# TensorE's program for 32 expert blocks written out without its loop

## The reference

```
p_g, g_idx = top_k(softmax(x @ w_group + b_group), 1)            # 1 of 4 groups
top_vals, top_idx = top_k(logits of the 8 experts of that group, 2)
weights = p_g * softmax(top_vals)
for each expert e of 32:  a, b = split(x @ w_gate_up[e], 2)      # 1024 -> 2 * 256
    out += gate[:, e] * ((silu(a) * b) @ w_down[e])              # 256 -> 1024
y = layer_norm(ALPHA * h + out)
```

## Time and profile before

| | us |
|---|---|
| median of 3 runs | 1188.25 (1187.29 to 1188.9) |
| the profiled execution's own time | 1186.87 |
| its span, first to last instruction | 1185.0 |
| outside the span | 1.87 |
| TensorE matmul busy | 1154.1 |
| VectorE busy | 739.8 |
| ScalarE busy | 597.2 |
| granted TensorE clock, mean | 0.996 |

### The profile page before, as it was taken

One profiled execution on the slowest core, in us unless ns is written; L12 is line 12 of the kernel. 1 busy time (PEld: TensorE's weight loads), 2 busy tenths in 40 slices (PEclk: granted clock), 3 DMA queues, 4 the chain that ended last, 5 costly groups with the idle time before them and its releaser, 6 DMA issues. The chain is left out here.

```text
span 1185.0 us, 20341 instructions
## 1 busy us (share of the span) xinstructions
PE 1154.1 (97%) x7145; PEld 1021.6 (86%) x7145; DVE 739.8 (62%) x1351; ACT 597.2 (50%) x1006; POOL 87.5 (7%) x91
## 2 busy tenths in 40 slices
PE   8999999999999999999989999899999999999997
PEld 8999999899999999999979899687788888878863
DVE  3326355365453653646655765656899999889955
ACT  3233344434344334343375732313688888888952
POOL 0000000000000000000000000011222222222113
PEclk9999999999999999999999999899999999999999
DMA  6623425325252152521523333732799999999916
GB/s 202 169 77 107 113 63 155 91 66 144 68 150 78 52 160 83 143 84 53 162 72 116 88 106 115 268 131 95 284 369 350 363 356 369 380 359 376 360 62 266
DMA packets 178476, 210.50 MB, mean 178 GB/s; under 512 B 14055, under 2 KB 141544, under 8 KB 178429
## 3 DMA queue, kind: packets, MB, share of 16 engines
q1 hardware_dynamic: 155440, 188.07, 48.0%
q10 hardware_dynamic: 13644, 10.77, 2.9%
q0 software_dynamic: 9344, 11.03, 2.7%
HBM read 200.19 MB, written 32.71 MB: 197 GB/s over the span
## 5 line engine op out<-in xcount | busy, mean ns | idle before, releaser
L345 PE MATMUL bank_u<-x_hi,w_hi 128*128 128x320 f32 (+1 forms) x1024 | 326.6, 319 | 0.4 <-DVE x_lo L776 0.4
L346 PE MATMUL bank_u<-x_lo,w_hi 128*128 128x320 f32 (+1 forms) x1024 | 318.9, 311 | 0.0
L347 PE MATMUL bank_u<-x_hi,w_lo 128*128 128x320 f32 (+1 forms) x1024 | 318.0, 311 | 0.0
L345 PEld LDWEIGHTS bank_u<-x_hi,w_hi 128*128 128x128 f32 x1024 | 192.5, 188 | 8.6 <-issue 7.1
L346 PEld LDWEIGHTS bank_u<-x_lo,w_hi 128*128 128x128 f32 x1024 | 192.9, 188 | 0.0
L347 PEld LDWEIGHTS bank_u<-x_hi,w_lo 128*128 128x128 f32 x1024 | 192.7, 188 | 0.0
L771 DVE TENSOR_TENSOR w_lo<-w_raw,w_hi 128x1024 fp32r<-128x1024 f32 x80 | 97.7, 1221 | 114.7 <-ACT w_hi L548 114.0
L548 ACT CAST w_hi<-w_raw 128x1024 fp32r<-128x1024 f32 x80 | 83.4, 1043 | 45.6 <-issue 28.4
L1527 PE MATMUL banks<-w_hi_space,xT_hi 128*128 128x512 f32 x256 | 102.6, 401 | 1.3 <-issue 1.2
L1528 PE MATMUL banks<-w_lo_space,xT_hi 128*128 128x512 f32 x256 | 99.8, 390 | 0.0
L1529 PE MATMUL banks<-w_hi_space,xT_lo 128*128 128x512 f32 x256 | 99.8, 390 | 0.0
(11 more groups left out here) (290 smaller groups left out, 2165.9 us busy)
## 6 DMA issues: line engine op xcount, KB each, us to landing
w_raw<-in_w_in SPq DMA_DIRECT2D x64, 512.0 KB, 4.1
first_up<-in_w_gate_up SPq DMA_DIRECT2D x16, 2048.0 KB, 12.3
second_up<-in_w_gate_up SPq DMA_DIRECT2D x16, 2048.0 KB, 12.3
first_down<-in_w_down SPq DMA_DIRECT2D x16, 1024.0 KB, 11.2
second_down<-in_w_down SPq DMA_DIRECT2D x16, 1024.0 KB, 11.1
k_cache<-in_cache_k SPq DMA_DIRECT2D x16, 512.0 KB
v_cache<-in_cache_v SPq DMA_DIRECT2D x16, 512.0 KB
w_raw<-in_w_branch SPq DMA_DIRECT2D x16, 512.0 KB, 4.3
```

The lines of the kernel that those rows point to most:

```text
L345: pe.matmul(out, w_hi[:, u % 2, k, :], x_hi[:, k, cols], start=(k == 0), stop=False)
L346: pe.matmul(out, w_hi[:, u % 2, k, :], x_lo[:, k, cols], start=False, stop=False)
L347: last = pe.matmul(out, w_lo[:, u % 2, k, :], x_hi[:, k, cols], start=False, stop=(k == KT - 1))
```

## The change

On TensorE alone, and for the first 32 blocks alone, `run` is replaced by a Python loop that calls `body` 32 times with whole numbers. So the 32 bodies are written out one behind the other: no counter, no branch, and constants in place of registers in the waits. The instructions that compute, their order, the semaphores and the values waited for are the same. The other engines keep their loops, and so does the code of the spare blocks.

```
@@ -1565,7 +1565,11 @@
                 turn_rows(j0 + 1, j0 // 2, 1)
                 if j0 == 0:
                     keep["keep_busy"](4)
-                run(pe, body, j0, j1)
+                if j0 == 0:
+                    for j in range(j1):
+                        body(j, j // 2, j % 2, j == 0, j1 - 1 - j)
+                else:
+                    run(pe, body, j0, j1)
                 down(j1 - 1, (j1 - 1) % 2)
```

## The result

| | before | changed |
|---|---|---|
| median, 15 runs each, taken together | 1187.38 (1185.88 to 1190.0) | 1185.84 (1183.98 to 1188.34) |
| ratio to the kernel before | 1 | 0.9985, 95% interval 0.9978 to 0.9992 |
| the profiled execution's own time | 1186.87 | 1186.06 |
| its span | 1185.0 | 1184.2 |
| turn_act of block 0 to that of block 31 | 294.40 | 293.47 |

The change makes the kernel faster by 1.8 us by the ratio (0.9 to 2.6). The forecast was 0.16 us (its 1188.1 also stood on a median of three runs, 0.9 us above that of fifteen). Two more measurements of the same program gave 0.9987 and 0.9986.

The account below looks back on a forecast made before the run. It took TensorE's matmuls as the bound from 898 to 992 and 1080 to 1127 us, and loads between; 0.76 us gained less 0.6 lost gave 0.16 us faster, a median of 1188.1 us, range 1185.8 to 1191.6.

Parts of the forecast that it names:

- 0.76 us gross and 0.16 net: Whole kernel: 0.35 us from block 6 plus 0.41 from blocks 24 and 26, less 0.6 for instruction packets.
- A late even block gains 0.36 us: TensorE, turn_act to gate_up of a late even block: falls from 0.68 to 0.32 us, as at late odd block 19.
- Five late even blocks, from one execution: TensorE's loop: only blocks 6, 20, 22, 24 and 26 show the branch, 0.60 to 0.69 us; eight others hide it.
- 0.35 for block 6: First TensorE-bound stretch: removing block 6's branch gains 0.35 us, from a range of 0.28 to 0.46.
- Blocks 20 and 22 are worth nothing, 24 and 26 together 0.41: 20 and 22, load-bound: 0.37 us each on TensorE, none kept; 24 and 26: 0.41 us if loads set act_rows(26).
- the chain of rows 2: What ended last, 992 to 1080 us: 61% second_up load, no matmul in front; TensorE savings there count only through starting it earlier.
- every late branch counts: Rival, whole loop: loads, splits and act_rows all follow TensorE, 2.0 us gained, fetch free, 1186.2 us; chance 0.12.
- 0.6 us for the packets: DMA queues: 9 or 10 added instruction packets, 3 or 4 in the load-bound stretch, cost 0.6 us, bounds 0 and 4.8.
- The slower rival: Load-bound stretch, 992 to 1080: 3 or 4 packets each delay a load's last piece 1.2 us; 1191.1 us; chance 0.22.
- No starving: TensorE's waits for its own instructions: taken as zero; the rival of 9 or 10 us lost, 1197.5, had chance 0.05.
- no change at the last jump: Jump over the spare blocks: 3.3 us, still covered by 4.4 us, unchanged.
- a taken branch costs a fetch: Rival, TensorE's loop: 12 branches back each cost a 1.2 us packet, 14 us in all, about 1174 us; chance 0.03.

Follow-up runs that it names:

- imitated: Changed kernel with six already-met semaphore instructions behind even blocks 4 to 28 and one behind odd blocks 3 to 27; 1187.6 us, ratio 1.000.
- first_out: Changed kernel with TensorE's blocks 19 to 28 back in the loop, 3 to 18 and 29 to 31 written out; 1186.28 us, 0.9992.
- before_again: Second profile of the unedited kernel before; 297.10 us from block 0 to 31.
- before_third: Third profile of the unedited kernel before; 293.91 us from block 0 to 31.
- standin: Changed kernel with four already-met semaphore instructions behind turn_act of each even block 4 to 28; 1186.43 us, 0.9989.
- long_pass: Changed kernel with TensorE's blocks 3 to 26 as a loop of two passes of 12 bodies, registers kept; 1185.96 us, 0.9987.
- last_out: Changed kernel with TensorE's blocks 3 to 18 back in the loop, 19 to 31 written out; 1186.31 us, 0.9988.
- again: Changed kernel measured and profiled a second time, no edit; 1186.21 us, 0.9987.
- again_third: Changed kernel measured and profiled a third time, no edit; 1185.97 us, 0.9986.
- three_out: Changed kernel with VectorE's and ScalarE's first 32 blocks written out as well as TensorE's; 1185.75 us, 0.9985.
- standin12: Changed kernel with twelve already-met semaphore instructions behind turn_act of each even block 4 to 28; 1192.34 us, 1.0044.

## Why the prediction was wrong

The sign was right by a hair, and so was the source of the gain: imitated shows that time on TensorE's sequencer is what the change removes, and the traces that it counts only where `act_rows` is late. What failed is how much of it reaches the end: 0.76 us gross and 0.16 net against 1.5 to 1.8 net. The measured 1185.84 lies at the very edge of my range (1185.8), and that edge stood on a median of the kernel before that was 0.9 us too high. By the steps:

- **A late even block gains 0.36 us.** Mis-sized. It is 0.42 to 0.51, 0.50 where `act_rows` comes last (0.69 to 0.19). The 0.32 us that I let stand for a block without a branch was block 19, an odd block that itself was in the loop and had register instructions ahead of `gate_up`; in the changed kernel late odd blocks have 0.19 too. The row contained some 0.1 us of what the change removes, and a late odd block gains this 0.1 us as well, which my sum put at nothing.
- **Five late even blocks, from one execution.** Mis-sized. "None" after the other eight was not even true of that execution: block 18 had 0.25 us and block 4 had 0.40, without the mark "issue" that I looked for:

```profile
888.11 0.38 PE L1537 MATMUL banks<-const_sb,act_rows 128*128 128x128 f32 x2
888.51 0.49 PE L1527 MATMUL banks<-w_hi_space,xT_hi 128*128 128x512 f32 x1
```

  And the next two profiles had seven and six marked gaps. 5 to 11 gained 0.62 us in the mean of three where I had 0.35 for block 6.
- **Blocks 20 and 22 are worth nothing, 24 and 26 together 0.41.** This is the step that carried most. I took the chain of rows 2, 61% load, as a wall behind which TensorE doesn't count, and `act_rows(26)` as set by the loads. But `act_rows` followed TensorE: from 21 to 29 the gaps behind `turn_act` (blocks 21 to 28, above 0.14 us each) are 1.69 us in the mean of the three looped profiles and 0.31 in the changed ones, 1.38 us less, and the stretch became 1.20 us shorter. Most of it reached the end, where I had let 0.41 through. That it counts in full isn't shown: first_out, looped there, had gaps of 1.31 us and took 76.24, and imitated had 1.43 and took 76.26, some 0.6 us less than the kernel before. For block 20 the case is open: 18 to 21 gained 0.53 us in the mean, but 0.16 without before_again.

  The loads followed as well. In SyncE's queue the down load of block 26 went out 4.19 us after the up load in the kernel before, and 3.80 us in the changed one; before, then changed:

```profile
1071.33 0.37 SPq L1467 DMA_DIRECT2D first_up<-in_w_gate_up  x1
1075.52 0.37 SPq L1469 DMA_DIRECT2D first_down<-in_w_down  x1
```

```profile
1071.95 0.37 SPq L1467 DMA_DIRECT2D first_up<-in_w_gate_up  x1
1075.75 0.37 SPq L1469 DMA_DIRECT2D first_down<-in_w_down  x1
```

  The other profiles bear this out. Where the gap behind block 22 was 0.56 us or more, in whatever program (before_third, first_out, standin, imitated), this distance was 4.12 to 4.23 us; where it was 0.38 or less (before_again, long_pass, last_out, again, again_third, three_out), it was 3.79 to 3.92. The same distance for block 24's loads, behind block 20, was 3.79 to 3.80 with or without a gap: there the wall held.

  A chain tells who came last; it doesn't tell that the last one was not itself started late by the engine I had ruled out. My rival "every late branch counts", 2.0 us gross, had 0.12 and was the nearest to what happened. By which engine the delay travels (ScalarE's copy is the likely way) is not shown.
- **0.6 us for the packets.** Their number was right, 9 or 10. The cost was too high if the copies of packets are a fair price, 0.27 us. The slower rival, 3.6 us, is out by that and by the load-bound stretch, which did not become longer with them.
- **No starving, no change at the last jump.** Right: no "issue" in TensorE's waits of the changed kernel from 860 to 1145 us.
- **What I had not in the sum at all:** blocks 0 to 5 took 0.77 us longer in the mean of three. Eight profiles in which TensorE has no branch behind block 4 and which are otherwise the changed kernel or near it had 47.7 to 49.0 us (the highest three_out), four of looped ones (the three of the kernel before, and last_out) 46.8 to 48.1, and again_third lies among both. Whether that is a cost of the change, for instance of its packets of instructions, or of a few draws stays open. If it is a cost, the gross gain is about 2.35 us, and my 0.6 us for the packets would not be far off after all.

The rival "a taken branch costs a fetch" was wrong, as I had thought: it would have brought 14 us. The Trainium skill ("Runtime: NRT & Kernel Launch", Instruction fetch mechanics) gives that stall as one reason why kernels prefer full unrolling. Here the looped kernel fetched nothing from 870 to 1118 us, and the unrolling was worth 1.5 to 1.8 us by another cause: long_pass gained the same with a loop.

## What to carry to other kernels

A branch at the end of a pass costs what is left of it after the lead of the last wait before it, that is after the time by which the data waited for was early: 0.5 us here where the data came just in time, nothing where it came 0.7 us early. So put a loop's end, if a choice is there, behind a wait that is met early, or make passes long; two passes of twelve bodies gave what the full writing-out gave, as far as the runs can tell. Before pricing such gaps take distances between starts in several executions, not the idle marks of one, compare with a block that lacks the removed instructions entirely, and don't write off an engine because the chain runs through another.

## What the runs showed of the hardware that I had not expected

- TensorE ran a pass of twelve bodies a second time without fetching it again. In long_pass the second pass of 12 bodies, 12 x 92 = 1104 matmul and weight-load instructions, ran from 984.0 to 1100.4 us, and its queues from 970 to 1100 show no packet of instructions:

```profile
L1571 PEldq COMPARE_BRANCH  x2: 82/153/224, 983.7 to 1100.4; - x2
...
q1 hardware_dynamic: 10707, 42.11, 86.6%
q0 software_dynamic: 3987, 6.12, 12.6%
```

  The branch that is taken costs 224 ns, the one that falls through 82.
- A semaphore instruction whose waits are already met has a recorded duration of 51 ns on TensorE's sequencer, but delays the next matmul by 0.09 to 0.10 us (four in standin, twelve in standin12), and two waits share one.
- The gaps behind the branches differ from one execution of the looped kernel to the next, in place and number: the 32 blocks took 293.91 to 297.10 us in three profiles, and 293.47 to 293.61 written out. That the written-out program is steadier is not shown: its 15 timed runs spread over 4.4 us, those of the kernel before over 4.1.
